# Delta rule: the smallest mask is multiplied by the strengths before the triangle is there

## The reference, cut to what matters

```
def gated_delta_chunked(q, k, v, g, beta, s0):
    q, k, v, g, beta = chunk(q), chunk(k), chunk(v), chunk(g), chunk(beta)
    gc = jnp.cumsum(g, axis=-1)
    ...
    kb = k * beta[..., None]
    vb = v * beta[..., None]
    lmat = jnp.where(strict, jnp.einsum('bhncd,bhnsd->bhncs', kb, k) * decay, 0.0)
    rhs = jnp.concatenate([vb, kb * jnp.exp(gc)[..., None]], axis=-1)
    sol = lax.linalg.triangular_solve(lmat, rhs, left_side=True, lower=True, unit_diagonal=True)
    ...
    def step(s, inp):
        qi, ki, ui, wi, gi, ai = inp
        v_new = ui - jnp.einsum('bhck,bhkv->bhcv', wi, s)
        ...
```

## Time and profile before

| | us |
|---|---|
| median of 3 runs | 4042.29 |
| lowest and highest of them | 4032.33, 4045.57 |
| the profiled execution | 4043.42 |
| its span in the trace | 4042.1 |
| TensorE busy, share of the span | 3683.3 (91%) |
| VectorE busy | 1654.0 (41%) |
| ScalarE busy | 1189.8 (29%) |
| GpSimd busy | 1362.9 (34%) |

### The profile page before, as it was taken

One profiled execution on the slowest core, in us unless ns is written; L12 is line 12 of the kernel. 1 busy time (PEld: TensorE's weight loads), 2 busy tenths in 40 slices (PEclk: granted clock), 3 DMA queues, 4 the chain that ended last, 5 costly groups with the idle time before them and its releaser, 6 DMA issues.

```text
span 4042.1 us, 72409 instructions
## 1 busy us (share of the span) xinstructions
PE 3683.3 (91%) x31788; PEld 2347.9 (58%) x31788; DVE 1654.0 (41%) x2930; ACT 1189.8 (29%) x2161; POOL 1362.9 (34%) x1215
## 2 busy tenths in 40 slices
PE   7997778999998988998899999899888888889998
PEld 3754565434444445555455555445676766748887
DVE  1345343234334121444523233643565656533344
ACT  3253222222112164333300000211456666420002
POOL 1320442002112112557433333334443434325444
PEclk9998787988899999989999999999999999989999
DMA  5430000620101211440111121132100000022222
GB/s 198 143 103 21 2 2 11 210 86 33 34 24 42 87 43 63 167 167 32 50 55 63 53 63 52 64 110 86 37 16 16 28 16 3 14 83 94 84 84 73
DMA packets 196419, 263.77 MB, mean 65 GB/s; under 512 B 6119, under 2 KB 151655, under 8 KB 194056
## 3 DMA queue, kind: packets, MB, share of 16 engines
q1 hardware_dynamic: 189168, 242.79, 18.2%
q10 hardware_dynamic: 6936, 16.35, 1.1%
HBM read 246.53 MB, written 12.58 MB: 64 GB/s over the span
## 4 chain that ended last, share of the span: by engine, by line
PE 74%; ACT 8%; DVE 6%; issue 5%; POOL 4%; DMA 1%; ACTq 0%; SPq 0%; DVEq 0%; POOLq 0%
PE ps L238 58%; PE ps L3071 3%; PE ps L764 2%; PE ps L382 1%; PE ps L489 1%; PE ps L779 1%; PE ps L791 1%; PE ps L2068 1%; ACT mem L841 1%; PE ps L498 1%; DVE mem L1225 1%; ACT mem L3006 1%; ACT mem L666 1%; POOL mem L2974 1%; PE ps L1386 1%
## 5 line engine op out<-in xcount | busy, mean ns | idle before, releaser
L238 PE MATMUL ps<-mem 64*64 64x64 f32 (+4 forms) x25184 | 2691.9, 302 | 163.9 <-ACT mem L666 33.1
L238 PEld LDWEIGHTS ps<-mem 64*64 64x64 f32 (+1 forms) x25184 | 1745.5, 155 | 1121.0 <-issue 576.3
L2974 POOL TENSOR_TENSOR mem<-mem 128x256 f32<-128x256 f32 (+1 forms) x264 | 225.8, 868 | 361.6 <-ACT mem L3483 179.1
L859 POOL TENSOR_SCALAR mem<-mem 128x768 f32<-128x768 f32 (+2 forms) x128 | 219.0, 1724 | 205.3 <-DVE mem L825 205.2
L2250 ACT ACTIVATE mem<-ps 128x384 f32<-128x384 f32 (+1 forms) x80 | 35.5, 445 | 778.6 <-PE ps L238 736.3
L2237 POOL TENSOR_TENSOR mem<-mem 128x512 f32<-128x512 f32 (+1 forms) x80 | 100.1, 1251 | 445.4 <-PE ps L238 368.4
L596 POOL TENSOR_TENSOR mem<-mem 128x512 f32<-128x512 f32 (+1 forms) x72 | 75.2, 1061 | 430.6 <-ACT mem L591 427.5
L2261 DVE TENSOR_TENSOR mem<-mem,ps 128x384 f32<-128x384 f32 (+1 forms) x80 | 39.9, 499 | 414.2 <-PE ps L238 414.2
L3071 PE MATMUL ps<-mem 128*128 128x128 f32 x960 | 179.2, 305 | 32.8 <-DVE mem L2996 20.1
L3004 ACT ACTIVATE mem<-ps 128x256 f32<-128x256 f32 (+1 forms) x220 | 101.4, 461 | 201.5 <-PE ps L3071 201.0
L2996 DVE TENSOR_TENSOR mem<-mem,ps 128x256 f32<-128x256 f32 (+1 forms) x220 | 109.7, 514 | 123.0 <-PE ps L238 122.2
(11 more groups left out here) (336 smaller groups left out, 4139.9 us busy)
## 6 DMA issues: line engine op xcount, KB each, us to landing
mem<-i_mod_w SPq DMA_DIRECT2D x48, 1024.0 KB, 6.9
mem<-i_ffn_wg SPq DMA_DIRECT2D x22, 1024.0 KB, 5.3
mem<-i_ffn_wu SPq DMA_DIRECT2D x22, 1024.0 KB, 5.3
mem<-i_e_w_in SPq DMA_DIRECT2D x16, 1024.0 KB, 6.1
mem<-i_o_w_in SPq DMA_DIRECT2D x16, 1024.0 KB, 5.6
mem<-i_ffn_wd SPq DMA_DIRECT2D x16, 1024.0 KB, 5.2
mem<-i_e_mod_w SPq DMA_DIRECT2D x12, 1024.0 KB, 11.8
mem<-i_o_mod_w SPq DMA_DIRECT2D x12, 1024.0 KB, 6.8
```

The costliest lines, as they stand in the source:

```text
L238: ins = e.h.matmul(out, l, r, start=(i == 0), stop=(i == n - 1))
L859: K.pool.h.tensor_scalar(w, w, stat(i, o, 1), None, MUL).then_inc(*nm.up(tag, i, o))
L2974: K.pool.h.tensor_tensor(m3(self.slot(l)), self.lraw, bm(C(K, f"cm{self.d}", l, 64), 2 * self.np), MUL).then_inc(*self.mk.up(key, l))
```

## The change

A third buffer for each lane, `SM[d]` of 256 columns, holds the mask of level 0 multiplied by the strengths of the unit. GpSimd writes it in `gates`, right behind the gate products of that unit, so at the end of the unit before, or, for the first unit, at the start of the scan.

When the two diagonal blocks are there, the mask of level 0 is one instruction, `Lc` times `SM`. Its wait is for the second of the two instructions of L1447 and no longer for L1448 as well. Only in the next turn does GpSimd multiply `Lc` in place by the strengths, wait for its own result, and write the mask of level 1 from it. `Inverse64.pool` takes two more arguments for that; its other caller, the scan of the second network, passes neither.

```
@@ delta_scan
     Xb = [[K.alloc(512) for _ in range(2)] for _ in range(2)]
+    SM = [K.alloc(256) for _ in range(2)]
@@ gates
         K.pool.h.tensor_tensor(h3(gm[d]), bc(G[:, tt, 4 * d:4 * d + 4], 128), tri(d), MUL).then_inc(*gate.up(d, i))
+        K.pool.h.tensor_tensor(m3(SM[d]), bm(C(K, f"cm{d}", 0, 64), 4), strength(d, tt, slice(0, 128), 128), MUL).then_inc(*scl.up(d, i, "first"))
@@ unit_pool
         yield
         yield
-        K.pool.wait_ge(*ux.at(d, i, "L"))
-        K.pool.h.tensor_tensor(m3(Lc[d]), m3(Lc[d]), strength(d, tt, slice(0, 128), 128), MUL).then_inc(*scl.up(d, i, "L"))
-        yield
-        steps = inv.pool([(scl, (d, i, "L"))])
+
+        def scaled():
+            K.pool.h.tensor_tensor(m3(Lc[d]), m3(Lc[d]), strength(d, tt, slice(0, 128), 128), MUL).then_inc(*scl.up(d, i, "L"))
+            K.pool.wait_ge(*scl.at(d, i, "L"))
+        steps = inv.pool([(ux, (d, i, "L", 1)), (scl, (d, i, "first"))], SM[d], scaled)
+        next(steps)
+        yield
         next(steps)
         yield
@@ Inverse64.pool
-    def pool(self, ready):
+    def pool(self, ready, first=None, scaled=None):
@@ masked
-            K.pool.h.tensor_tensor(m3(self.slot(l)), self.lraw, bm(C(K, f"cm{self.d}", l, 64), 2 * self.np), MUL).then_inc(*self.mk.up(key, l))
+            mask = bm(C(K, f"cm{self.d}", l, 64), 2 * self.np) if l or first is None else m3(first)
+            K.pool.h.tensor_tensor(m3(self.slot(l)), self.lraw, mask, MUL).then_inc(*self.mk.up(key, l))
         for sig, k in ready:
             K.pool.wait_ge(*sig.at(*k))
         masked(0)
+        if scaled:
+            yield
+            K.pool.wait_ge(*self.mk.at(key, 0))
+            scaled()
         masked(1)
```

## The result

| | before | changed |
|---|---|---|
| median of 18 runs each | 4039.2 us | 4025.0 us |
| lowest and highest | 4030.0, 4048.5 | 4008.2, 4037.1 |
| the profiled execution | 4043.4 | 4009.8 |
| its span | 4042.1 | 4008.5 |

The ratio is 0.9965, with a 95% interval from 0.9956 to 0.9975: 14 us less, where 7.1 were forecast. So 14 us is not the worth of the change everywhere, and part of what follows asks what differs.

The account below looks back on a forecast made before the run. The prediction took TensorE's waits for GpSimd's level-0 mask, and VectorE's for L1620, as the bound. Gains of 4.4 and 4.4 us less costs of 1.0 and 0.7 made 7.1 us less: 4035.2 us, range 4024 to 4047.

Parts of the forecast that it names:

- Which waits end last: In the lanes, TensorE waits twelve times, 29.1 us in total, for GpSimd's mask of level 0; forecast to fall near 9.4.
- Plain rounds: Units 0 and 1 of both lanes, four rounds: the mask starts 1.03 or 1.15 us sooner, 4.4 us gained.
- Chain rounds: Units 2 to 5, eight rounds: mask 1.91 us sooner, but the transpose only 0.50 or 0.59, 4.4 us gained.
- The new operation at the start: Start of the scan: two SM operations delay L1509 and the whole first unit, costing 1.0 us once.
- Collisions: VectorE's L1462 overlaps GpSimd's later mask in four rounds, costing 0.7 us; bounds 0 and, for eight rounds, 1.4.
- The other ten `SM` operations: Behind the gate products, before a mask of level 3: hidden by other steps, no cost; uncovered, up to 0.6 us each.
- The clock rises: Rival, chance 0.19: two more chain rounds at TensorE's high clock, 5 us each, bring 10 us on top: 4025.

Follow-up runs that it names:

- the second comparison: The changed kernel with no edit, measured once more against the kernel before for a second profile: 4029.3 us against 4027.7, ratio 0.9999.
- the kernel with both edits: The changed kernel with L1620 one turn earlier and SM written late, in the unit's own second turn: 4001.6 us against 4036.9 for the kernel before, ratio 0.9923.

## Why the prediction was right, and where its size was off

The steps of the waits were right, and the time lay inside the range. That it came out at 4025.0 owes something to luck: the change beyond the waits is one of TensorE's clock, and in the second comparison nothing was gained at all.

- *Which waits end last.* Right. TensorE's wait for the mask went to 9.3 us (forecast 9.4), and each of the 12 masks follows the second L1448 by 0.08 us.
- *Plain rounds, 4.4 us.* The waits are right to a tenth in laps 1 and 2 of the kernel with these rounds alone. The size of the whole term is off: that kernel gained 14 us. In the first profile of the changed kernel the first four laps are 8.7 us shorter, laps 3 and 4 at a higher granted clock; in the second, at the clock of before, 4.8 instead of 3.4. This is the mis-sized term.
- *Chain rounds, 4.4 us.* The mechanism is right in every step: the gain of 1.9 us is not passed on, the transpose waits for L2996 behind L1598 behind L1620, and comes 0.59 us sooner in lane 1 and 0.49 in lane 0 (506.30 to 509.20, before 522.12 to 525.51). VectorE's wait for the chain fell by eight times the 0.33 of this working, to 6.4; the 6 came from rounding. The total of these rounds alone shows no gain, and its interval leaves out the 3.7 that was expected. It allows the 4.4 less collisions of some 2 us. Whether that is the answer stays open.
- *The new operation at the start, 1.0 us.* 0.86 in the timeline, and 0.87 given back in lap 1 when it is written later.
- *Collisions, 0.7 us.* The mechanism is right, the size too small by about three: 2.6 and 1.9 us in the two profiles, with a longer pair in nine and eight of the twelve rounds. I had priced one overlap with one mask, 0.17 us; in the changed kernel L1463 runs beside `SM` and the mask one after the other, and the median of all 24 rose from 421 to 679 ns. By the rule of the Trainium skill (GPSIMD Engine Reference, Specifications), that GpSimd contends with a VectorE instruction with two inputs in SBUF, all eight rounds would count. The 1.4 us that the prediction gave for this was nearer.
- *The other ten `SM` operations, nothing.* No run tests this: a kernel with each of them done twice needs more columns than the kernel's buffer has, so it has no measured time. But the laps at equal clock are shorter by about what the waits say, which leaves no room for 0.6 us in each.
- *The clock rises.* I gave it 0.19 and put it into the chain rounds. In the first profile it came in the plain ones, and in the first two laps with the chain (18.0 and 19.7 us at 1.00 and 0.90, before 22.1 and 22.8 at 0.73 and 0.72). The 5 us for a round came from two windows in the earlier trace rows that are not laps; the laps there took 22.15 us at 0.95, 24.50 at 0.79 and 26.80 at 0.69. The reason given for the rise is not shown. The idle time that it names was cut in two in all eight chain rounds, and the last five of their laps took 119.45 and 119.33 us in the two profiles. They took 122.55 in the kernel before, but 117.86 in the same kernel with two extra matmuls. The rule of the Trainium skill (TensorE: Matmul & The Clock Gate, The HAM clock gate), that activity releases the throttle, agrees with the laps in its direction and does not say which laps; one filled gap in the kernel before took its own lap from 0.50 to 0.59 and no lap behind it higher.
- *The time.* 4025.0 lies in the range (4024 to 4047), near its low end, which only the rising clock reaches. By its own bands the first comparison belongs to the rival of the rising clock (0.19), since the forecast ended at 11 us less, and the second shows no gain. The forecast of 7.1 us less lies between the two, 14 and 0.

## What to carry to other kernels

When two streams share engines in a fixed order, follow an earlier result to the next instruction of the same queue: its gain ends where that instruction waits for the other stream. Here an operation moved ahead by 1.9 us gave 0.5, and moving the other stream's single operation (L1620, into idle time) gave 16 us by itself and 31 with the change (by the ratios, on one chip). And put a precomputed operand where its engine is known to wait, not where its inputs are first ready: in the trace this gave back 0.87 us at the start and, with L1620 in its place, most of the collisions, though no total shows it.

## What the hardware showed beyond what was expected

- In a stretch where TensorE works in short steps, savings of waits of some 3 to 15 us, by the expectations, moved the total by 14 to 31 us in six comparisons, and the mean granted clock of that stretch rose with it (0.63 to 0.80 in the first four laps, 0.79 to 0.90 in the others, in the kernel with both edits). In two other comparisons, of the chain rounds alone and of the changed kernel again, they moved nothing.
- In five comparisons, four of them known to be on different chips, the same kernel before had medians of 4027.7, 4034.3, 4036.3, 4036.9 and 4039.2 us. The first differs from the last by 11.5 us, nearly as much as the change was measured to gain, so at 0.3% kernels can be compared on the same chip only, and better on two.
- A VectorE operation of 64x256 with both inputs in SBUF takes 0.41 us alone and up to 0.90 beside GpSimd operations with two inputs.
- A quicker TensorE waits longer. For the same undisturbed pair L1463 of 0.87 us it waited 0.25 or 0.38 us at its low level and 0.50 or 0.63 at its high one. So part of what the high level gives comes back as waits.
